# Two transformer blocks on one core: the norms between stages rebuilt, with the root of four of them applied behind the up products

## The chip, the cores and the metric

The kernel runs on one core of one Trainium2 chip. The core's engines are TensorE (PE, with its weight loads PEld), VectorE (DVE), ScalarE (ACT), GpSimd (POOL) and SyncE (SP), which issues the DMAs. The metric is the device time of one launch in microseconds. The clock granted to TensorE (PEclk) is given as a share of its full 2.4 GHz.

## The reference

Inputs are x (256 tokens of width 1024), a conditioning vector c, and weights. All is in float32. What matters here:

```python
def rms_norm(x, g):
    return x * rsqrt(mean(x * x, -1) + EPS) * g

# first half: layers 0 and 1
mod = silu(c) @ ada_w[l] + ada_b[l]              # 9 vectors of 1024 for each layer
h = rms_norm(x, g) * (1 + sc1) + sh1
x = x + 0.5 * g1 * swiglu(h)                     # feed-forward, 1024 -> 2 x 2816 -> 1024
h = ...;  x = x + g2 * (hybrid(h) if l == 0 else nsa(h))
h = ...;  x = x + 0.5 * g3 * swiglu(h)
# between the halves
x = rms_norm(x, final_g)
# second half: layers 0 and 1
f = (silu(rms_norm(x, g_pre) @ w_gate) * (rms_norm(x, g_pre) @ w_up)) @ w_down
x = x + 0.5 * rms_norm(f, g_post)
x = x + rms_norm(conformer(h) if l == 0 else diff_attention(h), g_post)   # h = rms_norm(x, g_pre)
x = x + 0.5 * rms_norm(f, g_post)                # a second feed-forward
```

There are 12 stages with a product in them: six in the first half (norms 0 to 5, feed-forwards 0 to 3, a hybrid of convolution and attention, an nsa attention) and six in the second (norms 6 to 11, feed-forwards 4 to 7, a conformer convolution, a differential attention). Norms 6, 8, 9 and 11 stand ahead of feed-forwards 4, 5, 6 and 7.

## The kernel before

Activations are kept with features on the partitions: `x`, `hf`, `h_hi` and `h_lo` are 128 x 8 chunks x 256 tokens. Weights come from memory as slabs of 128 x 2048 (1 MB), through three slots `raw`, `hi`, `lo`. ScalarE copies `raw` to `hi` in the rounded type of the matmuls, VectorE subtracts to get the rest `lo`, and every product is three matmuls (`mm3`): hi by hi, hi by lo, lo by hi. The activations are split the same way. Each engine runs its own program in a fixed order written out by hand, and semaphores join them. At the end of a stage `ahead()` splits the next stage's first two slabs, in front of the add.

A feed-forward has 11 steps. A step takes a gate slab and an up slab (`up`, into the two PSUM banks `AB[:, A]` and `AB[:, B]`, 48 matmuls each), and the down slab of the step before (`down`, into `Y`, 48 matmuls). ScalarE applies silu to bank A as soon as both banks are done, VectorE multiplies by bank B (`gate_mul`), and both split the product into `g_hi` and `g_lo` (in the last step `z_hi` and `z_lo`). The first step's `up` goes through the chunks of the first slab as they become ready; then four matmuls with zeros clear `Y` (L552), and the next `up` waits for the first gate product. In feed-forwards 0 to 3 VectorE also works on the ada product: `mac` multiplies 2 MB of weights by c (eight operations over 512 columns, L1256 and L1259), `cols` on TensorE sums over the partitions (L481), and `mod_out` stores the result. Pair `q0` is done before step 1, the others at the ends of the steps.

A norm goes so: ScalarE squares eight chunks into `hf` (L911; L974 for the result in `Y`; L979), GpSimd adds them in pairs (L845), and TensorE multiplies each pair sum by a column of ones, for the two halves of the tokens into banks `M` and `N` (L499). That is the statistic. VectorE computes the root with a seed from the bits and three Newton steps of three operations each (`rsqrt`, L1324 to L1329), TensorE spreads it over the partitions into `N` (L504, four records), and VectorE multiplies chunk by chunk (L1366), ScalarE writes `h_hi`, VectorE writes `h_lo` (L1372, L1376). An `add` of the second half norms the result of the stage too: statistic over `Y`, root, spread, a copy of the spread to `rstd` (L1346), and then for each chunk `hf = (Y + bias) * rstd` (L1452) and `x = x + gate * hf` (L1458). The `gate` vector is written by VectorE at the start of the add (L1440). In the conformer GpSimd makes diagonal matrices (L855) after the pairs of norm 7.

The start of the add and of the norm on VectorE:

```python
                rstd_of(EPS)
                for k in range(KD + 1):
...
                        ins = nc.vector.scalar_tensor_tensor(hf[:, k, :], Y[:, k, :], bias, rstd[:, :],
                                                             ALU.add, ALU.mult)
```

## Time and profile before

| what | value |
|---|---|
| time, median of 3 runs | 2496.24 us (2495.17 to 2500.86) |
| span of the profiled execution | 2499.1 us (its own time is not listed apart from the span) |
| PE busy | 2260.6 us, 90% |
| DVE busy | 1496.0 us, 60% |
| ACT busy | 924.7 us, 37% |
| POOL busy | 128.4 us, 5% |
| mean granted TensorE clock | 0.926 |
| HBM read | 415.2 MB, 167 GB/s over the span |

The profile is of one execution. Times in rows are microseconds from the span's start unless marked ns. An operation's row gives start, duration, engine, line, and output and inputs by their names; in square brackets stands how long the engine had been idle before it and what released it. Matmuls overlap, so the time from one start to the next says more than a duration. An f32 matmul of the statistic or the spread shows as two records.

### The profile page before, as it was taken

Reading aid. Unit: us, or ns where it says so; the run is one execution under the profiler, and the core shown is the slowest. Engines: PE = TensorE matmul, PEld = TensorE weight load, DVE = VectorE, ACT = ScalarE, POOL = GpSimd, SP = SyncE. Lnnn points to the kernel's source line nnn. Section 1 sums busy time; section 2 is a strip of 40 time slices with the busy share of each in tenths; the row PEclk is TensorE's granted clock in tenths of the full one; section 3 lists DMA queues with packets and bytes.
Section 4 is the critical chain, followed back from the end, with each engine's and each line's share of the span. In section 5 each row is a group of like instructions: output and inputs, shape, how many; then the busy total and the mean of one; then the engine's idle time right before and its main releaser. Section 6 shows DMA issues by size and latency. Waiting matters only on the chain.

```text
span 2499.1 us, 41640 instructions
## 1 busy us (share of the span) xinstructions
PE 2260.6 (90%) x17518; PEld 2208.7 (88%) x17518; DVE 1496.0 (60%) x2025; ACT 924.7 (37%) x1161; POOL 128.4 (5%) x92
## 2 busy tenths in 40 slices
PE   3999868999999999999989988779998998977997
PEld 3999768999899898889979988779997997967997
DVE  7776765776776536574454458954445446475444
ACT  2333433333333444343433333133343433433332
POOL 0000000000000000000000014510000001001000
PEclk9999888999999878899989988879998998988999
DMA  7776432776575332045525542115552552502552
GB/s 277 277 287 250 169 125 112 287 291 263 218 298 223 140 115 84 34 169 185 185 104 185 184 149 85 68 53 183 185 185 102 184 185 110 185 10 86 185 184 84
DMA packets 52499, 417.42 MB, mean 167 GB/s; under 512 B 5824, under 2 KB 5952, under 8 KB 6208
## 3 DMA queue, kind: packets, MB, share of 16 engines
q1 hardware_dynamic: 52416, 416.27, 44.8%
q8 instruction: 57, 0.93, 0.1%
q14 instruction: 26, 0.21, 0.0%
HBM read 415.20 MB, written 1.05 MB: 167 GB/s over the span
## 4 chain that ended last, share of the span: by engine, by line
PE 83%; DVE 12%; ACT 2%; issue 2%; POOL 1%; DMA 1%; SPq 0%; DVEq 0%; POOLq 0%; ACTq 0%
PE AB L252 17%; PE AB L253 17%; PE AB L254 17%; PE Y L252 8%; PE Y L254 8%; PE Y L253 8%; DVE lo L1230 2%; PE Y L660 2%; DVE ada_acc L1259 1%; PE M L481 1%; PE N L504 1%; PE M L691 1%; POOL hf L845 1%; DVE qT L1730 1%; PE Y L675 1%
## 5 line engine op out<-in xcount | busy, mean ns | idle before, releaser
L1230 DVE TENSOR_TENSOR lo<-raw,hi 128x2048 fp32r<-128x2048 f32 x322 | 747.1, 2323 | 591.4 <-ACT hi L883 591.2
L252 PE MATMUL AB<-h_hi,hi 128*128 128x256 f32 x3328 | 970.7, 292 | 27.7 <-DVE h_lo L1372 11.1
L253 PE MATMUL AB<-h_lo,hi 128*128 128x256 f32 x3328 | 956.1, 287 | 0.0
L254 PE MATMUL AB<-h_hi,lo 128*128 128x256 f32 x3328 | 955.3, 287 | 0.0
L883 ACT ACTIVATE hi<-raw 128x2048 fp32r<-128x2048 f32 x322 | 613.9, 1910 | 574.9 <-PE Y L254 303.4
L252 PEld LDWEIGHTS AB<-h_hi,hi 128*128 128x128 f32 x3328 | 651.3, 196 | 37.3 <-issue 19.5
L253 PEld LDWEIGHTS AB<-h_lo,hi 128*128 128x128 f32 x3328 | 654.7, 197 | 0.1
L254 PEld LDWEIGHTS AB<-h_hi,lo 128*128 128x128 f32 x3328 | 653.6, 196 | 0.0
L252 PE MATMUL Y<-g_hi,hi 128*128 128x256 f32 x1280 | 362.2, 283 | 0.0
L253 PE MATMUL Y<-g_lo,hi 128*128 128x256 f32 x1280 | 362.2, 283 | 0.0
L254 PE MATMUL Y<-g_hi,lo 128*128 128x256 f32 x1280 | 362.2, 283 | 0.0
L252 PEld LDWEIGHTS Y<-g_hi,hi 128*128 128x128 f32 x1280 | 245.8, 192 | 0.0
L253 PEld LDWEIGHTS Y<-g_lo,hi 128*128 128x128 f32 x1280 | 245.8, 192 | 0.0
L254 PEld LDWEIGHTS Y<-g_hi,lo 128*128 128x128 f32 x1280 | 245.8, 192 | 0.0
L1259 DVE SCALAR_TENSOR_TENSOR ada_acc<-ada_raw,cact,ada_acc 128x512 f32<-128x512 f32 x245 | 185.6, 758 | 8.7
L845 POOL TENSOR_TENSOR hf<-hf 128x256 f32<-128x256 f32 x80 | 68.3, 862 | 2312.8 <-ACT hf L911 1100.6
L1384 DVE TENSOR_TENSOR gf<-silu,AB 128x512 f32<-128x512 f32 x88 | 60.3, 685 | 193.3 <-ACT silu L949 133.2
L949 ACT ACTIVATE silu<-AB 128x512 f32<-128x512 f32 x80 | 47.8, 597 | 331.7 <-PE AB L254 331.7
L499 PE MATMUL M<-ones,hf 128*128 128x1 f32 x166 | 38.4, 300 | 49.4 <-POOL hf L845 47.9
L499 PEld LDWEIGHTS M<-ones,hf 128*128 128x128 f32 x166 | 32.8, 246 | 56.7 <-POOL hf L845 55.2
L481 PEld LDWEIGHTS M<-one,ada_acc 128*128 128x128 f32 x288 | 39.7, 211 | 46.1 <-DVE ada_acc L1259 30.1
L481 PE MATMUL M<-one,ada_acc 128*128 128x1 f32 x288 | 38.9, 256 | 44.7 <-DVE ada_acc L1259 44.7
(270 smaller groups left out, 2337.6 us busy)
## 6 DMA issues: line engine op xcount, KB each, us to landing
raw<-slabs SPq DMA_DIRECT2D x322, 1024.0 KB, 4.8
ada_raw<-ada SPq DMA_DIRECT2D x35, 2048.0 KB, 8.1
x<-x_t SPq DMA_DIRECT2D x1, 1024.0 KB, 10.2
kT<-ada SPq DMA_DIRECT2D x1, 1024.0 KB, 18.6
vt<-ada SPq DMA_DIRECT2D x1, 1024.0 KB, 20.6
out_t<-x SPq DMA_DIRECT2D x1, 1024.0 KB, 3.9
vec<-vectors SPq DMA_DIRECT2D x1, 462.0 KB, 3.5
hf<-constants SPq DMA_DIRECT2D x1, 401.0 KB, 15.2
```

Of the source, the lines that this page charges most:

```text
L252: nc.tensor.matmul(out_, w_hi, r_hi, start=start, stop=False, **kw)
L253: nc.tensor.matmul(out_, w_hi, r_lo, start=False, stop=False, **kw)
L254: return nc.tensor.matmul(out_, w_lo, r_hi, start=False, stop=stop, **kw)
L481: mm = nc.tensor.matmul(M[:, j:j + 1], ada_acc[:, j * P:(j + 1) * P], one[:, 0:1], start=True, stop=True)
L499: mm = nc.tensor.matmul((M, N)[t][:, 0:1], hf[:, base + every * k, t * P:(t + 1) * P], ones_[:, 0:1], start=(k == 0), stop=(k == n_chunks ...
L660: nc.tensor.matmul(out_, q_ap, k_ap, start=True, stop=not bias)
L845: nc.gpsimd.tensor_tensor(hf[:, k, :], hf[:, k, :], hf[:, k + 1, :], ALU.add).then_inc(pair_ready, 1)
L883: nc.scalar.activation(hi[slot][:, :], raw[slot][:, :], ACT.Copy).then_inc(hi_done[slot], 1)
L949: nc.scalar.activation(silu[:, :], AB[:, A, :], ACT.Silu).then_inc(silu_done, 1)
L1230: nc.vector.tensor_tensor(lo[slot][:, :], raw[slot][:, :], hi[slot][:, :].bitcast(F32), ALU.subtract).then_inc(lo_done[slot], 1)
L1259: nc.vector.scalar_tensor_tensor(ada_acc[:, :], w[k], cact[:, k:k + 1], ada_acc[:, :], ALU.mult, ALU.add).then_inc(ada_mac, 1)
L1384: nc.vector.tensor_tensor(gf[:, :], silu[:, :], AB[:, B, :], ALU.mult).then_inc(gf_done, 1)
```

## The change

- **Statistic.** GpSimd's four pair sums become a tree: chunks 0 to 3 are summed into one, 4 and 5 into one, 6 and 7 stay apart (`tree`). TensorE takes four parts (`stat_tree`): the sum of four, the sum of two, and the last two squares. Both token halves go to columns of one bank, `M`. Norms 7 and 10 are summed by TensorE from all eight squares, without GpSimd (`stat(KD, ones[1024])`).
- **Root.** `root_of` reads both columns at once; each Newton step is two operations instead of three, done for each token half by an instruction of its own.
- **Adds of the second half.** ScalarE squares each bank of `Y` into `ysq` (which is `kT`) and then writes `hf = gate * Y` for that bank; for this it waits once for VectorE's gate vector. VectorE multiplies `hf` by the spread, which it reads from `N` with no copy, and adds to `x`. The final norm reads `N` too.
- **Deferred norms** (6, 8, 9 and 11). `h = x * g` without the root: ScalarE writes `h_hi` from `x`, then the square; VectorE writes `h_lo` in the loop of the add (`low_half`). A reduction on VectorE sums the squares over chunks (`square_sum`), TensorE sums over the partitions after the first two slabs, the root follows, and its spread stands between the halves of the third slab. In every step VectorE multiplies both up products by the root (`gate_scaled`), and ScalarE's silu reads the scaled one.
- **First slabs.** In all stages the first two slabs are multiplied together, chunk by chunk (`by_chunk`). In feed-forwards they go into banks of `Y`. The next `up` no longer waits for the first gate product, and the first `down` starts the sums in `Y`, with no matmuls by zero.
- **Order.** In step 1 of a feed-forward the next up slab is split ahead of silu and the gate product. `mac` and `mod_out` stand between the gate product and the split of the down slab, in every step; the first `mac` is in step 1, and `cols` comes one step later.
- **Output.** Four DMAs of two chunks each instead of one.

```diff
+        DEFERRED = (6, 8, 9, 11)
+        def y_bank(b):
+            return Y[:, 2 * b:2 * b + 2, :].rearrange("p k t -> p (k t)")
 SyncE:
+                for k in range(0, KD, 2):
+                    sp.wait_ge(x_new, c["x_new"] - KD + k + 2)
+                    sp.dma_start(out[:, k:k + 2, :], x[:, k:k + 2, :]).then_inc(stored, 16)
 TensorE:
+            def stat_tree(sq):
+                s0, p0 = c.take("sq", KD), c.take("pair", 4)
+                sums([(pair_ready, p0 + 3, sq[:, 0, :]), (pair_ready, p0 + 4, sq[:, 4, :]),
+                      (sq_ready, s0 + 7, sq[:, 6, :]), (sq_ready, s0 + 8, sq[:, 7, :])], ones[1024])
+                spread()
+            def by_chunk(banks):
+                js = [c.take("slab") for _ in banks]
+                for k in range(KD):
+                    wait_h(k)
+                    for j, bank in zip(js, banks):
+                        s_ = j % 3
+                        if k == 0:
+                            pe.wait_ge(lo_done[s_], j // 3 + 1)
+                        for cc in range(2):
+                            at = k * 2 * P + cc * P
+                            mm = mm3(bank[:, cc * T:(cc + 1) * T], hi[s_][:, at:at + P], lo[s_][:, at:at + P],
+                                     h_hi[:, k, :], h_lo[:, k, :], k == 0 and cc == 0, k == KD - 1,
+                                     skip_group_check=True)
+                        if k == KD - 1:
+                            mm.then_inc(used[s_], 1)
             def ffn(f):
-                for ab in range(2):
-                    j = c.take("slab")
-                    pe.wait_ge(lo_done[j % 3], j // 3 + 1)
-                    up(ab == 0, ab, j % 3)
-                for b in range(4):
-                    nc.tensor.matmul(Y[:, 2 * b:2 * b + 2, :].rearrange("p k t -> p (k t)"), zero_b[:, 0:P],
-                                     zero_b[:, :], start=True, stop=False, skip_group_check=True)
+                by_chunk([y_bank(0), y_bank(1)])
+                if f >= 4:
+                    sums([(acc_ready, f - 3, rstd)], ones[1024])
+                pe.wait_ge(lo_done[ring[0][0]], ring[0][1] + 2)
+                up(0, ring[0][0], between=spread if f >= 4 else None)
+                pe.wait_ge(lo_done[ring[1][0]], ring[1][1] + 2)
+                up(1, ring[1][0])
+                pe.wait_ge(lo_done[ring[2][0]], ring[2][1] + 2)
+                pe.wait_ge(glo_done, g0 + 1)
+                down(ring[2][0], first=True)
 GpSimd:
+            def tree(sq):
+                pool.wait_ge(sq_ready, s0 + 2)
+                nc.gpsimd.tensor_tensor(sq[:, 0, :], sq[:, 0, :], sq[:, 1, :], ALU.add).then_inc(pair_ready, 1)
+                pool.wait_ge(sq_ready, s0 + 4)
+                nc.gpsimd.tensor_tensor(sq[:, 2, :], sq[:, 2, :], sq[:, 3, :], ALU.add).then_inc(pair_ready, 1)
+                pool.wait_ge(pair_ready, p0 + 2)
+                nc.gpsimd.tensor_tensor(sq[:, 0, :], sq[:, 0, :], sq[:, 2, :], ALU.add).then_inc(pair_ready, 1)
+                pool.wait_ge(sq_ready, s0 + 6)
+                nc.gpsimd.tensor_tensor(sq[:, 4, :], sq[:, 4, :], sq[:, 5, :], ALU.add).then_inc(pair_ready, 1)
+                if kind == "norm" and a[0] >= 6:
+                    c.take("sq", KD)
 ScalarE:
             def norm(n):
+                if n in DEFERRED:
+                    for k in range(KD):
+                        act.wait_ge(x_new, c["x_new"] - KD + k + 1)
+                        nc.scalar.activation(h_hi[:, k, :], x[:, k, :], ACT.Copy, scale=g[:, k:k + 1]
+                                             ).then_inc(hh_ready, 1)
+                        nc.scalar.activation(hf[:, k, :], x[:, k, :], ACT.Square).then_inc(sq_ready, 1)
+                    return
             def add(n):
+                    for b in range(KD // 2):
+                        result_bank(act, c, n, b)
+                        for k in (2 * b, 2 * b + 1):
+                            nc.scalar.activation(ysq[:, k, :], Y[:, k, :], ACT.Square, bias=bias).then_inc(sq_ready, 1)
+                        if b == 0:
+                            act.wait_ge(gate_done, n - 5)
+                        for k in (2 * b, 2 * b + 1):
+                                nc.scalar.activation(hf[:, k, :], Y[:, k, :], ACT.Copy, scale=gate[:, k:k + 1]
+                                                     ).then_inc(yg_ready, 1)
 VectorE:
+            def root_of(eps, scale=None):
+                link(nc.vector.tensor_scalar(vh, M[:, 0:TT], eps, -0.5, ALU.add, ALU.mult))
+                link(nc.vector.tensor_scalar(root[:, :].bitcast(I32), vh.bitcast(I32), -0.5, RSQRT_SEED,
+                                             ALU.mult, ALU.add))
+                for step in range(3):
+                    for t in range(TT):
+                        nc.vector.scalar_tensor_tensor(tmp[:, t:t + 1], y, y, vh[:, t:t + 1], ALU.mult, ALU.mult
+                                                       ).then_inc(dve_link, 1)
+                    for t in range(TT):
+                        dve.wait_ge(dve_link, at + t + 1)
+                        nc.vector.scalar_tensor_tensor(y, tmp[:, t:t + 1], 1.5, y, ALU.add, ALU.mult)
+            def gate_scaled(g, a_bank, b_bank, slot_b, n_b):
+                dve.wait_ge(used[slot_b], n_b)
+                dve.wait_ge(glo_done, g)
+                for to, from_ in ((silu, a_bank), (gf, b_bank)):
+                    nc.vector.tensor_tensor(..., from_, rstd broadcast, ALU.mult)
+                dve.wait_ge(silu_done, g + 1)
+                nc.vector.tensor_tensor(gf[:, :], gf[:, :], silu[:, :], ALU.mult).then_inc(gf_done, 1)
             def step(...):
+                    if first:
+                        split(sb_, i + nb)
+                    if first and f >= 4:
+                        dve.wait_ge(rstd_ready, c["stat"])
+                        link(nc.vector.tensor_copy(rstd[:, :], N[:, 0:T]))
                     gate_scaled(...) or gate_mul(...)
+                    if not first:
+                        split(sb_, i + nb)
+                    if out_:
+                        mod_out(i + (q0 - 2))
+                    if mac_:
+                        mac(0, i + (q0 - 1), i + (a0 - 1))
                     split(sw, i + nw)
                     gate_lo(i + (g0 - 1))
-                    if out_:
-                        mod_out(i + (q0 - 1))
                     if a:
                         split(sa, i + (na + 1))
-                    if mac_:
-                        mac(0, i + q0, i + a0)
             def add(n):
+                rstd_of(EPS, copy=False)
+                for k in range(KD + 2):
+                    if k < KD:
+                        nc.vector.tensor_tensor(hf[:, k, :], hf[:, k, :], N[:, 0:T], ALU.mult)
+                    if 1 <= k <= KD:
+                        nc.vector.tensor_tensor(x[:, k - 1, :], x[:, k - 1, :], hf[:, k - 1, :], ALU.add)
+                    if n + 1 in DEFERRED and k >= 2:
+                        low_half(n + 1, k - 2)
```

## Rows read from the trace of the kernel before

**Rows 1.** The page: granted clock in 40 slices, and the chain that ended last
```profile
PEclk9999888999999878899989988879998998988999
...
PE 83%; DVE 12%; ACT 2%; issue 2%; POOL 1%; DMA 1%; SPq 0%; DVEq 0%; POOLq 0%; ACTq 0%
```

**Rows 2.** Windows: stretch, length, busy us by engine, PEclk, DMA share, GB/s
```profile
1268.30:1288.00 19.70, 8.76 (x42) 7.58 (x41) 11.76 (x43) 6.46 (x17) 6.14 (x8) 0.62 0.16 64
1655.40:1676.30 20.90, 8.42 (x41) 7.34 (x40) 12.57 (x45) 4.98 (x12) 4.55 (x6) 0.58 0.11 45
1871.30:1891.70 20.40, 8.46 (x42) 7.39 (x41) 12.21 (x45) 4.80 (x12) 4.41 (x6) 0.56 0.15 60
1891.70:1906.20 14.50, 14.50 (x97) 14.39 (x97) 6.94 (x14) 4.31 (x7) 0.00 (x0) 0.79 0.20 73
2268.10:2288.00 19.90, 7.95 (x42) 6.94 (x40) 12.24 (x45) 4.80 (x12) 4.35 (x6) 0.63 0.12 49
1302.20:1470.00 167.80, 167.18 (x1390) 166.41 (x1390) 79.27 (x49) 65.41 (x49) 0.00 (x0) 1.00 0.50 181
```

**Rows 3.** Timeline of PE, between feed-forwards 5 and 6
```profile
1872.97 0.38 PE L499 MATMUL M<-ones,hf 128*128 128x1 f32 x2 [0.32 <-POOL hf L845]
1873.21 0.36 PE L499 MATMUL N<-ones,hf 128*128 128x1 f32 x2
1875.93 1.22 PE L504 MATMUL N<-ident,root 128*128 128x128 f32 x4 [2.36 <-DVE root L1329]
...
1882.48 0.59 PE L499 MATMUL M<-ones,hf 128*128 128x1 f32 x2 [0.58 <-POOL hf L845]
1882.93 0.57 PE L499 MATMUL N<-ones,hf 128*128 128x1 f32 x2
```

**Rows 4.** Timeline of DVE, the same stretch
```profile
1867.65 2.29 DVE L1230 TENSOR_TENSOR lo<-raw,hi 128x2048 fp32r<-128x2048 f32 x1 [0.18 <-ACT hi L883]
1869.86 0.71 DVE L1440 TENSOR_SCALAR gate<-vec 128x8 f32<-128x8 f32 x1
...
1877.19 0.42 DVE L1346 COPY rstd<-N 128x256 f32<-128x256 f32 x1 [1.31 <-PE N L504]
...
1878.32 0.47 DVE L1458 SCALAR_TENSOR_TENSOR x<-hf,gate,x 128x256 f32<-128x256 f32 x1
1878.72 0.42 DVE L1452 SCALAR_TENSOR_TENSOR hf<-Y,rstd 128x256 f32<-128x256 f32 x1
1879.05 0.48 DVE L1458 SCALAR_TENSOR_TENSOR x<-hf,gate,x 128x256 f32<-128x256 f32 x1
```

**Rows 5.** Timeline of ACT, the last squares of the add there
```profile
1871.46 0.66 ACT L974 ACTIVATE hf<-Y 128x256 f32<-128x256 f32 x2 [0.78 <-PE Y L254]
```

**Rows 6.** Timeline, where the last down product of feed-forward 3 begins
```profile
1261.57 0.69 DVE L1388 TENSOR_TENSOR z_lo<-gf,z_hi 128x512 fp32r<-128x512 f32 x1
...
1262.49 0.28 PE L252 MATMUL Y<-z_hi,hi 128*128 128x256 f32 x1
```

**Rows 7.** Timeline of PE, feed-forward 4 behind its first 96 matmuls
```profile
1302.27 1.04 PE L552 MATMUL Y<-zero_b 128*128 128x512 bf16 x4
1303.92 0.39 PE L252 MATMUL AB<-h_hi,hi 128*128 128x256 f32 x1 [0.62 <-DVE gf L1384]
```

**Rows 8.** Timeline, norm 7: a diagonal beside a Newton step
```profile
1499.38 2.56 POOL L855 TENSOR_TENSOR ot<-ident,vec 128x1408 f32<-128x1408 f32 x1
1499.48 2.47 DVE L1327 TENSOR_TENSOR var<-var,root 128x2 f32<-128x2 f32 x1
```

**Rows 9.** Timeline of DVE, feed-forward 1 ahead of step 1
```profile
432.75 5.48 DVE L1259 SCALAR_TENSOR_TENSOR ada_acc<-ada_raw,cact,ada_acc 128x512 f32<-128x512 f32 x7
```

**Rows 10.** The page: DMA issues, KB each, us to landing
```profile
out_t<-x SPq DMA_DIRECT2D x1, 1024.0 KB, 3.9
```

**Rows 11.** The chain near the program's start: start us, us, what
```profile
21.13 1.11 DVE ada_acc L1259
```

**Rows 12.** Groups of DVE in the differential attention, 2112 to 2265
```profile
L1786 DVE TENSOR_REDUCE rec<-hf 128x8 f32<-128x1024 f32 x2 | 2.4, 1220 | 0.1
```

More of the change, by code:

```diff
@@ L275, in program @@
                     for kind, *_ in plan)
+        SQ_DONE, n_sq = {}, 0
+        for kind, *a in plan:
+            if kind in ("norm", "final", "conformer") or kind == "add" and a[0] >= 6:
+                n_sq += KD
+            elif kind == "hybrid":
+                n_sq += 3
+            if kind == "norm":
+                SQ_DONE[a[0]] = n_sq
         ADA_FFN = {0: (4, 10), 1: (16, 10), 2: (26, 8), 3: (34, 2)}
@@ L614, in features @@
                     for k in range(KD):
[L615 removed]
+                        if paced and cc == 0:
                             wait_h(k)
@@ L753, in nsa @@
             def nsa():
-                for j in range(4):
-                    features(halves(result("a")), first=(j == 0))
+                by_chunk([result("a"), result("a")])
+                for j in (2, 3):
+                    features(halves(result("a")))
                 for j in (4, 5):
@@ L861, in _ @@
                     diagonals()
-                if kind in ("norm", "final", "conformer") or kind == "add" and a[0] >= 6:
-                    pairs()
+                if kind == "norm" and a[0] >= 6:
+                    c.take("sq", KD)
+                elif kind in ("norm", "final", "conformer"):
+                    tree(hf)
+                elif kind == "add" and a[0] >= 6:
+                    tree(ysq)
                 elif kind == "hybrid":
```

261 lines of the change are left out of this document (158 added, 103 removed).

## The prediction

> **What bounds the kernel now.** I read the page first. The chain that ended last is 83% TensorE and 12% VectorE, and the granted clock falls to eight or seven tenths in the slices where one stage gives way to the next [rows 1]. The windows say why. Inside the feed-forward loops TensorE is busy 167.2 of 167.8 us at the full clock, while VectorE does 79 us of work, so what is put on VectorE there lies beside matmuls. Between stages it is the reverse: from the last product of one stage to the first of the next 19.7, 20.9, 20.4 and 19.9 us pass before the four feed-forwards of the second half, with TensorE busy about 8 us of it, and on tiny matmuls [rows 2]. Then the PE and VectorE timelines of one such stretch (1871 to 1892): statistic, root, spread, copy, an add at 0.73 us a chunk, a second statistic, root and spread, and only then the first product [rows 3, 4].
>
> **The sum by stages.** I count from the last product of a stage (E) to the first of the next (S), from S to the end of its first 96 matmuls (F), and from F on.
>
> *Pieces that recur.* (a) Root: 2.36 us pass between statistic and spread [rows 3], for two evictions, a seed and nine dependent steps. The new chain has one eviction, a seed and three times two steps, each step a pair of small instructions that overlap; a dependent step costs 0.2 us (2.36 over 12, with the ends), the second of a pair about 0.08. That makes 1.9: -0.4 each. (b) The copy of the spread, 0.46 us with its wait [rows 4], goes in adds and in the final norm. (c) Statistic after the tree. GpSimd still makes four adds in a row, 0.77 us each (eight in 6.14 us [rows 2]), and the last ends when it did; but now three parts wait behind it in place of one. A part is two matmuls, 0.24 us apart at 2.4 GHz and 0.45 at 1.2 GHz [rows 3], so two more parts cost 0.9 or 1.8: I take +1.25. (d) In the adds of the second half the last two squares go straight to TensorE, without a GpSimd hop: -0.75 where banks come late. (e) But ScalarE now also scales each bank, and waits at bank 0 for the gate, which VectorE writes only at 1870.57, behind two slab splits [rows 4]. Twelve operations of 0.33 us [rows 5] then follow, so the last square ends near 1874.6 in place of 1872.1. With the next item the statistic of an add behind a feed-forward ends 2.0 later (not in the last add: no slab is split ahead there). (f) The last product of a feed-forward: z_lo ends 0.23 us before TensorE wants it [rows 6]; the scaling of the up products in front of it takes 0.7, so TensorE stands 0.6; this is within the +2.0.
>
> *Deferred norms.* The new norm waits for no second statistic: x, then h_hi on ScalarE, then h_lo. After the spread come three VectorE operations of 0.33 to 0.48, one of 0.42 on ScalarE and one more on VectorE: S is 2.45 us behind the spread (1.55 after the final norm, with one VectorE operation less). So E to S becomes:
> - before the second (after the conformer): 0.9 last squares + 0.5 + 1.9 + 1.2 spread + 2.45 = 7.0, against 20.9: -13.9.
> - third: 4.35 to the statistic's end (2.35 now, + 2.0 by (e)) + 1.9 + 1.2 + 2.45 = 9.9, against 20.4: -10.5.
> - fourth: 7.0 (spread nearer to 0.8), against 19.9: -13.0.
> - first: 4.8 to the statistic's end (3.9 now; (c) at full clock, +0.9) + 1.9 + 1.2 + 1.55 = 9.5, against 19.7: -10.2.
>
> Behind S the clock is at 1.2 GHz, as before: TensorE has then stood about as long as it did when the clock fell. The 96 matmuls take 14.5 us at a mean clock of 0.79 [rows 2], so 0.12 each at full clock, nearly twice that at half, and the clock rises some 6 us behind S. Chunk-outermost order gives TensorE 12 matmuls per chunk (1.44 us at full clock, over 2.5 at half) against a supply of one chunk per 1.1 us on VectorE (three operations), so it never waits for a chunk. But before, it did three per 0.73 us where three at half clock take 0.64 to 0.7: it hardly waited, and there is little to win. F is S + 14.0 against 14.5 [rows 2]: -0.3 to -0.6. At F the clearing matmuls and the wait for the first gate cost 1.65 us [rows 7]; now the sums (0.45) and the spread (0.7) stand there: -0.5 (last: -0.85, estimated). The reduction over the squares, the next slab's split and the root lie beside the 14 us; if that cover were gone, they would cost 2.2 + 2.3 + 1.9 a time. Together: first -11.0, second -14.9, third -11.5, fourth -14.2.
>
> *Inside those four loops.* Per step (`gate_scaled`) VectorE gets two more operations over 512 columns, 0.69 each like the z_lo of [rows 6], and the gate comes 2.9 us behind the up products (scale 0.7, silu 0.6 beside the second scale, product 0.7, with waits) in place of 1.5. The 48 down products, 5.8 us, lie between: nothing. VectorE's 9.7 us a step fit into TensorE's 17.3. Unseen is the price of such a product with a broadcast operand; bounds are 0.69 and, as in the stretched row of [rows 8], 2.5. At the upper one the chain is 2 x 2.5 + 0.7 and some waits, and just fills the cover. I take 0.69, the row with one operand in PSUM and the same shape.
>
> *First half.* In step 1 the ada accumulation now stands between the first gate product and the next split. From F: hi 2.0, split 4.3, gate 4.95, eight accumulations of 0.75 [rows 9] to 10.95, split 13.15, g_lo 13.85; TensorE is through its next two slabs at 11.5: it stands 2.4. The clearing matmuls and wait of 0.9 go: +1.5. In later steps g_lo is ready 15.9 us after the gate chain starts and due at 18.1. Stage by stage: first feed-forward +0.6 (chunk-outermost must also wait for the second slab, but an old stall of 6.5 us goes), hybrid 1.25 (c) - 0.4 (a) + 0.05 - 0.75 for its own two roots = +0.15; the second feed-forward 1.25 - 0.4 - 0.9 (F) + 1.5 = +1.45; the third the same with F at -0.5, +1.85; nsa 1.25 - 0.4 - 0.6 + 0.75 = +1.0 (both result banks end together, so the third slab waits 0.75 for a ScalarE copy); the fourth with F at -0.8, +1.55. Sum +6.6.
>
> *The rest.* Norm before the conformer: GpSimd's diagonals (2.56 each) hold VectorE's root for 3.4 us now [rows 8]; they only move ahead, to the root of the add before, since GpSimd has no squares to wait for there any more. Conformer: its two first results end together, so its taps, which bound it, start 2.9 later; with (e), (c) and what is saved +1.3 in all. Diff: +0.4. Last add: statistic -0.75 + 0.6, root and copy -0.85, adds -0.35, and the output in four pieces instead of one of 3.9 us [rows 10]: -1.5; sum -2.9.
>
> Total: 6.6 - 11.0 + 1.3 - 14.9 - 11.5 + 0.4 - 14.2 - 2.9 = -46.2 us. The profiled execution spans 2499.1, so 2452.9 in such an execution; its span lies 2.9 above the median of the three runs, so 2450 for a median.
>
> **A rule against the change.** In [rows 4] the product that reads PSUM (L1452) lets its successor start after 0.33 us, no later than the one with all inputs in SBUF does (L1458, 0.40). The Trainium skill, VectorE: DVE Perf Modes, section on the TRN2 errata, gives VectorE 58 cycles of fixed cost from SBUF and 120 from PSUM. By that each of the products that now read the spread from PSUM would pay some 0.065 us more (an estimate from that page), 0.5 an add: the copy's saving would be gone, 3 us in all. The row decides here.
>
> **Rivals.**
> - *The clock does not fall* in the shorter pauses. For it: they shrink from 20 us to 7 to 10. Against it: in [rows 3] the spread, 4.8 us behind the last product, already runs at 1.2 GHz (1.22 us for four). Worth 28 x 0.09 = 2.6 us each and more for the spreads: about 2439.
> - *The accumulation comes too late in every first-half step.* Slack is 2.2 us. If an accumulation takes 1.1 us rather than 0.75, as at the start of the program [rows 11], TensorE stands 0.6 in 27 steps: 2466.
> - *The reduction is slow.* It reads 2048 elements with a stride. Nearest row: 1.22 us for 1024 in order [rows 12], so 2.2 to 2.4. At four times that it and the splits behind it end some 5 us after F: 4 x 5, so 2470.
> - *Slower.* The gate chain of the deferred loops becomes the bound: it decides from the point where the chain from the up products to the gate exceeds the 5.8 us of down products. To end above 2496 each of 40 steps must stand 1.2 us, so the chain must take 7.0, over twice my 2.9; with both scalings at the stretched 2.5 it is 5.8, not enough. With all three products at 2.5 it is 7.6, TensorE stands 1.8 in each step, and the time is 2450 + 72 = 2522. For it: the two last products have two operands in SBUF. Against it: GpSimd, beside which the stretched row ran, is idle in these loops [rows 2].
> - *It does nothing on the path*: the deferred products still wait for the root. Only if the order on VectorE put the root ahead of the chunks; it stands behind them. 2492.
>
> **How the numbers follow.** Forecast 0.64 (own range 2440 to 2460, from (c), (e) and where the clock rises), clock 0.09, accumulation 0.10, reduction 0.08, slower 0.04, nothing 0.05. The predicted time is that of the first; low 2436 takes in the clock, high 2468 the accumulation and most of the reduction. A measurement here tells 0.2% (5 us) from nothing. Faster: 0.64 + 0.09 + 0.10 + 0.08 + 0.02 = 0.93; same 0.03 (2492 lies near the bound, so its 0.05 is shared 2 to 3); slower 0.04.
>
> **What would show it.** First products before the four feed-forwards 7 to 10 us behind the last one; no clearing matmuls; first gate at F without a stop of TensorE in the second half and a stop of 2.4 us before the first down product in the first half; last statistic three parts long; ScalarE waiting for the gate at bank 0; root 1.9. It is wrong if TensorE's idle time in the second-half loops grows, or if the clock rises much later than 6 us behind S.

## The result and the profile after

The changed kernel takes 2531.18 us in the median of 4 runs (2526.72 to 2541.8), the kernel before 2495.99 beside it. The ratio is 1.015, with a 95% interval of 1.0128 to 1.0171: slower by 1.5%, where I forecast 2450 us and a gain. The profiled execution spans 2524.9 us, 25.8 more than that of before; my sum said 46.2 less.

By the end of the last product of each stage, the 25.8 come from opposite sides. The first half, up to feed-forward 3, is 65.8 us longer (forecast: 6.6). Its feed-forwards lost 25.3, 23.5, 18.5 and 6.3 us, with 10, 10, 8 and 2 ada accumulations; hybrid and nsa gained 1.6 and 6.3. The second half is 39.9 us shorter (forecast: 52.8): feed-forwards 4, 5, 6 and 7 gained 9.4, 9.7, 10.1 and, with the end, 13.3 us (forecast: 11.0, 14.9, 11.5 and 17.1); the conformer lost 2.9 and diff gained 0.3.

The page of the kernel after, its chain that ended last (to be read against [rows 1]):

```profile
PE 59%; DVE 20%; DMA 10%; ACT 5%; issue 4%; POOL 1%; SPq 1%; DVEq 0%; ACTq 0%
PE AB L259 10%; PE AB L261 10%; PE AB L260 10%; DMA raw<-slabs 10%; DVE ada_acc L1357 7%; PE Y L259 6%; PE Y L260 6%; PE Y L261 6%; DVE lo L1328 4%; ACT hi L954 4%; DVE qT L1903 2%; PE M L524 2%; PE Y L721 2%; PE Y L736 1%; PE M L752 1%
```

TensorE had 83% of that chain before and has 59% now. New in it are slab loads (10%) and the accumulation (7%). The waits after, first PE's, then ACT's, then those of SP's queue (us in total, times, longest):

```profile
PE Y L259 <- DVE g_lo L1535: 53.0, 30, 2.9
...
ACT hi L954 <- DMA raw<-slabs: 249.2, 53, 10.5
...
SPq L418 <- DVE lo L1328: 1822.4, 292, 101.9
SPq L428 <- DVE ada_acc L1357: 462.4, 29, 30.1
```

and SP's in the kernel before:

```profile
SPq L392 <- DVE lo L1230: 2050.5, 318, 109.0
SPq L402 <- DVE ada_acc L1259: 207.8, 29, 29.5
```

Read them from the bottom up. SP issues every load, in one fixed order. Its 29 ada loads used to wait 207.8 us for accumulations; they now wait 462.4. ScalarE then waits 249.2 us for slabs, a wait that is in none of the longest of before, and TensorE stands 30 times, 53.0 us, ahead of a down product. There are 30 accumulations in the feed-forwards: one stop for each. Four of the stops are in first steps, 1.5 us each; 26 are in later steps.

One such step, in feed-forward 1. The chain that ended last, 480 to 503, then DVE, SP, ACT and PE, then the step as a window (length, busy us by engine, PEclk, DMA share, GB/s):

```profile
472.45 9.33 DMA raw<-slabs
481.81 1.92 ACT hi L954
...
493.10 10.73 DMA raw<-slabs
```

```profile
483.75 2.29 DVE L1328 TENSOR_TENSOR lo<-raw,hi 128x2048 fp32r<-128x2048 f32 x1 [6.80 <-ACT hi L954]
...
486.03 0.48 DVE L1354 TENSOR_SCALAR ada_acc<-ada_raw,cact 128x512 f32<-128x512 f32 x1
486.55 5.48 DVE L1357 SCALAR_TENSOR_TENSOR ada_acc<-ada_raw,cact,ada_acc 128x512 f32<-128x512 f32 x7
491.94 2.28 DVE L1328 TENSOR_TENSOR lo<-raw,hi 128x2048 fp32r<-128x2048 f32 x1
494.14 0.68 DVE L1535 TENSOR_TENSOR g_lo<-gf,g_hi 128x512 fp32r<-128x512 f32 x1
...
505.80 2.29 DVE L1328 TENSOR_TENSOR lo<-raw,hi 128x2048 fp32r<-128x2048 f32 x1 [8.17 <-ACT hi L954]
...
492.22 0.33 SPq L428 DMA_DIRECT2D ada_raw<-ada  x1
493.10 4.43 SPq L418 DMA_DIRECT2D raw<-slabs  x3
...
503.86 1.91 ACT L954 ACTIVATE hi<-raw 128x2048 fp32r<-128x2048 f32 x1 [10.53 <-DMA raw<-slabs]
...
494.97 0.36 PE L259 MATMUL Y<-g_hi,hi 128*128 128x256 f32 x1 [2.28 <-DVE g_lo L1535]
```

```profile
480.13:502.28 22.15, 19.87 (x154) 19.70 (x153) 13.63 (x14) 6.86 (x5) 0.00 (x0) 0.92 0.67 267
```

The split of slab b at 483.75 ends at 486.04 and frees its slot, so the reload could start. But SP's next entry is the ada load, and that waits for the accumulation behind the split. It goes out at 492.22, the slab's reload at 493.10, 7 us late and behind 2 MB of ada weights, so that it needs 10.73 us, where the median of all slab loads is 4.8. ScalarE gets the slab at 503.86 after 10.53 us of nothing, VectorE splits it at 505.80, and the accumulation of that step starts as late again. The accumulation does not take longer (5.48 for seven, as in [rows 9]). It begins late, and g_lo is 2.28 us late with it. Then comes the clock: the step's mean is 0.92. Its 22.15 us are 4.0 more than the 18.16 that a step takes in e1 below, 2.3 by standing and the rest by half clock.

This step is not the usual one. From one `g_lo` to the next the first three feed-forwards take 20.4 to 20.9 us in 24 of 25 cases, with the slab's load at 9.2 to 9.6; the one of 22.1 is where that load takes 10.73. Later in the same feed-forward TensorE stands as long, at full clock (the row of one stop, and the step behind it up to the end of the next stop):

```profile
599.52 0.36 PE L259 MATMUL Y<-g_hi,hi 128*128 128x256 f32 x1 [2.48 <-DVE g_lo L1535]
...
599.50:620.10 20.60, 18.41 (x153) 18.26 (x153) 13.66 (x15) 6.86 (x5) 0.00 (x0) 1.00 0.64 258
```

So what sets the pace is a ring without TensorE in it: the ada load goes out, 0.9 us later the slab load (9.3), then come ScalarE's copy (1.9), VectorE's split (2.3), the accumulation (6.1), and the next ada load. It takes 20.6 us against TensorE's 18.2.

### The profile page after: what moved, and what is told of

The parts are those of the page before. It is cut to its first block, busy times and chain, and to the rows that moved or that the text cites. A ratio compares the mean times of both kernels' runs of the same rounds, so it can differ in the third digit from the quotient of the medians.

```text
span 2524.9 us, 41719 instructions
## 1 busy us (share of the span) xinstructions
PE 2252.9 (89%) x17470; PEld 2207.7 (87%) x17470; DVE 1547.4 (61%) x2128; ACT 946.2 (37%) x1209; POOL 113.2 (4%) x68
## 4 chain that ended last, share of the span: by engine, by line
PE 59%; DVE 20%; DMA 10%; ACT 5%; issue 4%; POOL 1%; SPq 1%; DVEq 0%; ACTq 0%
PE AB L259 10%; PE AB L261 10%; PE AB L260 10%; DMA raw<-slabs 10%; DVE ada_acc L1357 7%; PE Y L259 6%; PE Y L260 6%; PE Y L261 6%; DVE lo L1328 4%; ACT hi L954 4%; DVE qT L1903 2%; PE M L524 2%; PE Y L721 2%; PE Y L736 1%; PE M L752 1%
## 5 line engine op out<-in xcount | busy, mean ns | idle before, releaser
L259 PE MATMUL AB<-h_hi,hi 128*128 128x256 f32 x3072 | 880.7, 287 | 12.6 <-DVE ada_raw L1913 5.8
L260 PE MATMUL AB<-h_lo,hi 128*128 128x256 f32 x3072 | 875.1, 285 | 0.0
L261 PE MATMUL AB<-h_hi,lo 128*128 128x256 f32 x3072 | 874.8, 285 | 0.0
L954 ACT ACTIVATE hi<-raw 128x2048 fp32r<-128x2048 f32 x322 | 614.6, 1910 | 645.3 <-DMA raw<-slabs 249.2
L260 PEld LDWEIGHTS AB<-h_lo,hi 128*128 128x128 f32 x3072 | 595.9, 194 | 0.1
L259 PE MATMUL Y<-h_hi,hi 128*128 128x256 f32 x512 | 156.3, 305 | 27.0 <-DVE h_lo L1469 8.4
L260 PE MATMUL Y<-h_lo,hi 128*128 128x256 f32 x512 | 154.0, 301 | 0.0
L261 PE MATMUL Y<-h_hi,lo 128*128 128x256 f32 x512 | 153.4, 300 | 0.0
L259 PEld LDWEIGHTS Y<-h_hi,hi 128*128 128x128 f32 x512 | 108.1, 211 | 29.7 <-DVE h_lo L1469 9.5
L260 PEld LDWEIGHTS Y<-h_lo,hi 128*128 128x128 f32 x512 | 108.1, 211 | 0.0
L261 PEld LDWEIGHTS Y<-h_hi,lo 128*128 128x128 f32 x512 | 107.7, 210 | 0.0
## 6 DMA issues: line engine op xcount, KB each, us to landing
x<-x_t SPq DMA_DIRECT2D x1, 1024.0 KB, 10.1
vt<-ada SPq DMA_DIRECT2D x1, 1024.0 KB, 20.4
```

Source lines behind the costliest of these rows:

```text
L259: nc.tensor.matmul(out_, w_hi, r_hi, start=start, stop=False, **kw)
L260: nc.tensor.matmul(out_, w_hi, r_lo, start=False, stop=False, **kw)
L261: return nc.tensor.matmul(out_, w_lo, r_hi, start=False, stop=stop, **kw)
L954: nc.scalar.activation(hi[slot][:, :], raw[slot][:, :], ACT.Copy).then_inc(hi_done[slot], 1)
```

## Experiments

All times are medians, all ratios against the kernel before, run beside them on the same chip. Runs e1 to e4 share one chip, e5 to e8 a second, e9 and e10 a third; across these groups the ratios compare better than the times.

| run | us | ratio, 95% interval |
|---|---|---|
| e1_load_order | 2460.32 | 0.9841 (0.9817 to 0.9864) |
| e2_old_accumulation | 2456.66 | 0.9826 (0.9810 to 0.9843) |
| e3_before_new_accumulation | 2565.64 | 1.0267 (1.0246 to 1.0287) |
| e4_gate_early | 2520.96 | 1.0082 (1.0065 to 1.0099) |
| e5_both_mended | 2447.09 | 0.9798 (0.9768 to 0.9827) |
| e6_pairs | 2436.81 | 0.9759 (0.9735 to 0.9782) |
| e7_not_deferred | 2482.46 | 0.9955 (0.9936 to 0.9973) |
| e8_slab_order | 2449.40 | 0.9807 (0.9784 to 0.9831) |
| e9_chunk_order_where_deferred | 2431.24 | 0.9734 (0.9714 to 0.9754) |
| e10_squares_first | 2428.16 | 0.9727 (0.9707 to 0.9747) |

### The loss of the first half: e1, e2, e3

**e1**, in SP's program of the changed kernel:

```diff
                 def step(i, ada, a):
                     load(sb_, i * 3 + (j0 - 2), i + nb)
+                    if ada:
+                        load_ada(0, i + (q0 - 1), i * KD + KD * (q0 - 1))
                     load(sw, i * 3 + (j0 - 1), i + nw)
                     if a:
                         load(sa, i * 3 + j0, i + (na + 1))
-                    if ada:
-                        load_ada(0, i + q0, i * KD + KD * q0)
...
-                for flags, run in groupby(range(1, NSTEP), lambda i: (i < n_ada, i < NSTEP - 1)):
+                for flags, run in groupby(range(1, NSTEP), lambda i: (2 <= i <= n_ada, i < NSTEP - 1)):
```

> The changed kernel with one edit in SP's list of loads: in a feed-forward step the load of the modulation slab stands behind the load of slab b and ahead of those of w and a, as the subtractions and the accumulation now follow each other on DVE, instead of behind all three. Theory (the modulation load, which waits for the accumulation that now lies in the middle of DVE's step, holds up the reload of slab b behind it in SP's queue by about 6.5 us): the steps with modulation go from 22.15 us back to about 18.2, the three waits of some 2.3 us a step go, and with the 1.7 us that stay in each first step the time is about 2527 - 60 = 2467 us (2460 to 2475). Rival one (the accumulation itself is too late for the product of the same step, the slack of 2.2 us that the prediction left being too small, whatever SP does): the wait for g_lo stays at some 1.8 us in 28 steps and the time is 2505 to 2527. Rival two (the loads of other queues or the DMA engines' share are short): nothing moves, 2527.

2460.32 us: the theory, at the lower edge of its range, and 71 us below the changed kernel by the medians (68.6 by the profiled spans), by one entry moved in one queue. PE's wait for g_lo in the whole kernel, and one step of feed-forward 1 as a window:

```profile
PE Y L259 <- DVE g_lo L1535: 6.0, 4, 1.5
```

```profile
481.66:499.82 18.16, 18.16 (x154) 18.16 (x153) 13.88 (x15) 7.68 (x6) 0.00 (x0) 1.00 0.78 300
```

The 26 stops outside the first steps are gone, with 47.0 us of waiting; the four in first steps stay, at 1.5. Up to the last product of feed-forward 3 the trace is 67.25 us shorter. In TensorE's time that is the 47 of standing and 20 of half clock, which had stood behind 12 of the 26 stops; in cause it is the ring, some 2.45 us a step in 26 steps, an estimate of 64 us. The two don't add to each other, for where the clock had fallen the next stop was mostly shorter (2.22 us, then 1.04, in feed-forward 0) and the pace was the same. That half now takes 1.5 us less than before the change. The rival that the slack of 2.2 us was too small falls: the same order on VectorE, with loads on time, lets TensorE run through.

**e2**: `mac`, `cols` and `mod_out` at their old places, and with them `mac(0, q0, a0)` ahead of step 1. VectorE's part, without its loop bounds:

```diff
-                    if out_:
-                        mod_out(i + (q0 - 2))
-                    if mac_:
-                        mac(0, i + (q0 - 1), i + (a0 - 1))
                     split(sw, i + nw)
                     gate_lo(i + (g0 - 1))
+                    if out_:
+                        mod_out(i + (q0 - 1))
                     if a:
                         split(sa, i + (na + 1))
+                    if mac_:
+                        mac(0, i + q0, i + a0)
```

> The changed kernel with the modulation's accumulation, its columns and its read-out put back where they were before (one accumulation ahead of the first step, then at the end of each step); SP's list is untouched, and all else of the change stays. Theory (the whole loss of the first half hangs on where the accumulation stands): both that loss of 66 us and the wait of 1.7 us in each first step go, about 2527 - 66 = 2461 us (2452 to 2468). Rival (the chunk-outermost first slabs, the written-out first step or the statistic cost part of the first half): 2470 or more, with the rest of the loss left in the feed-forwards of the first half. The second half should stay as it is in the changed kernel, 40 us shorter than before.

2456.66 us, as the theory has it, and within 4 us of e1, which their intervals do not tell apart. What the new place was good for can't be seen in the time: with either order in agreement with SP's, the loops run at TensorE's pace.

**e3**: the same lines the other way round, put into the kernel before.

> The kernel before with that one part of the change: the accumulation, its columns and its read-out at their new places on DVE and PE, SP's list untouched. Theory: it alone makes the loss, 2497 + 60 = 2557 us (2545 to 2570), with steps of about 22 us in the first three feed-forwards. Rival (the loss needs the new first step or the slabs in chunk order as well): 2497 to 2515.

2565.64 us, inside the theory's range and 2.7% slower than before, with nothing else of the change. The wait is the same one in the same number:

```profile
PE Y L252 <- DVE g_lo L1388: 56.5, 30, 2.9
```

So the place of the accumulation, against an SP list that was not moved with it, is both needed for the loss and enough for it.

### The second half: e4 and e5

From here on a product's end is its start plus the 0.12 us to the next start. The add behind the conformer in the changed kernel; ACT, DVE, POOL, PE, with the last product ending at 1714.65:

```profile
1710.90 0.82 ACT L1063 ACTIVATE kT<-Y,vec 128x256 f32<-128x256 f32 x2
1714.19 1.02 ACT L1068 ACTIVATE hf<-Y,gate_bias,gate 128x256 f32<-128x256 f32 x2 [2.46 <-DVE gate_bias L1604]
...
1718.33 0.90 ACT L1063 ACTIVATE kT<-Y,vec 128x256 f32<-128x256 f32 x2
...
1711.03 2.29 DVE L1328 TENSOR_TENSOR lo<-raw,hi 128x2048 fp32r<-128x2048 f32 x1 [3.47 <-ACT hi L954]
1713.24 0.71 DVE L1603 TENSOR_SCALAR gate<-vec 128x8 f32<-128x8 f32 x1
...
1711.81 2.12 POOL L907 TENSOR_TENSOR kT<-kT 128x256 f32<-128x256 f32 x1 [32.98 <-ACT kT L1063]
1716.02 0.72 POOL L909 TENSOR_TENSOR kT<-kT 128x256 f32<-128x256 f32 x1 [2.10 <-ACT kT L1063]
...
1723.35 1.22 PE L533 MATMUL N<-ident,root 128*128 128x128 f32 x4 [2.19 <-DVE root L1450]
1726.81 0.58 PE L259 MATMUL Y<-h_hi,hi 128*128 128x256 f32 x1 [2.24 <-DVE h_lo L1469]
```

ScalarE stands 2.46 us for the gate, behind a mixer too. Its last two squares end at 1719.2, 4.6 us behind the last product, where I had put 0.9. In e4 the gate vector is written at the start of the stage (`gate_vector`, with the lines taken from the start of `add`; its definition is left out here):

```diff
                 step(1, y_bank(0), y_bank(1), (j0 - 1) % 3, (j0 - 1) // 3 + 1, False, n_ada > 0, True, first=True)
+                if f >= 4:
+                    gate_vector(3 * (f // 2) + 2 * (f % 2))
...
             def conformer():
+                gate_vector(7)
...
             def diff():
+                gate_vector(10)
```

> The changed kernel with one edit: in the second half the gate vector is written at the start of the stage and not behind DVE's splits for the next one. Theory (each addition's scaled copies, and behind them the last squares, wait about 2.5 us for the gate, behind the mixers too, which the prediction left out): each of the six additions ends its statistic 2 to 2.5 us sooner, about 2527 - 13 = 2514 us (2510 to 2517), and E to S becomes about 7.5 to 8 us in all three feed-forward to mixer transitions. Rival (the squares then wait for the copies between them, or POOL's tree is what ends last): 0.5 to 1 us for each, 2521 to 2525.

2520.96 us, 10 below the changed kernel. That misses the theory's 2510 to 2517 and lies at the rival's 2521. The trace says otherwise about the size: the second half is 12.8 us shorter than in the changed kernel, the theory's 13, while the first half of this execution is 9.6 longer, with no edit there and a cause that stays open. From the last product to the first the second, third and fourth feed-forward now take 8.66, 8.92 and 8.51 us, after 12.16, 11.26 and 10.22; ahead of the conformer and diff 1.6 less each. That is not the 7.5 to 8 I wrote, and e4's rows of the same add say why; it is what the rival named, the copies between the squares and the tree:

```profile
1721.99 1.08 ACT L1068 ACTIVATE hf<-Y,gate_bias,gate 128x256 f32<-128x256 f32 x2
1722.89 0.91 ACT L1063 ACTIVATE kT<-Y,vec 128x256 f32<-128x256 f32 x2
...
1722.62 2.18 PE L524 MATMUL M<-ones,kT 128*128 128x1 f32 x16 [0.66 <-POOL kT L911]
```

The last product ended at 1721.80, but its squares wait for the copies of the bank before (until 1722.89), and then two of the four parts are still to come at half clock, until 1724.8.

**e5** has the edits of e1 and e4.

> The changed kernel with the load order of e1 and the early gate vector of e4 together. Theory (two causes in different halves, which add up): 2460 - 10 = 2450 us (2446 to 2454). Rival (the early gate vector gives part back, as the first step of a feed-forward has less room once the loads are on time): 2454 to 2460.

2447.09 us: the two causes add up. This is the change as it could have been, near my 2450, in part by luck. By halves the trace has +4.4 and -51.2 us against my +6.6 and -52.8, but the terms err both ways: the stretches from last product to first are 10.4, 8.7, 8.5 and 8.7 us where I had 9.5, 7.0, 9.9 and 7.0.

### The statistic: e6

e5 with pair sums on GpSimd and four parts, each as its pair is ready:

```diff
-                sums([(pair_ready, p0 + 3, sq[:, 0, :]), (pair_ready, p0 + 4, sq[:, 4, :]),
-                      (sq_ready, s0 + 7, sq[:, 6, :]), (sq_ready, s0 + 8, sq[:, 7, :])], ones[1024])
+                sums([(pair_ready, p0 + k + 1, sq[:, 2 * k, :]) for k in range(4)], ones[1024])
```

> e5 with the statistic's tree put back to pair sums (four sums of two on GpSimd, four parts on TensorE, each as its pair is ready; both token halves stay in one bank). Theory (the tree's tail of three parts on TensorE, which lasts 2.05 us from 1925.6 to 1927.64 in the trace of e4, costs more than a last sum of 0.73 and one part of 0.7 behind the last square): 0.9 us less for each of 13 statistics, 2438 us (2434 to 2444). Rival one (the sum's term (c) was 0.9 to 1.8 only beside late squares, and the squares and GpSimd set the end either way): 2447 to 2452. Rival two (the tree is the better order where squares come late, as the change has it): 2453 or more.

2436.81 us, as the theory has it; the two intervals overlap a little, so the rows carry the rest. The statistic between feed-forwards 5 and 6, on PE, in e5 (last product until 1854.31):

```profile
1854.89 2.28 PE L524 MATMUL M<-ones,kT 128*128 128x1 f32 x16 [0.43 <-POOL kT L911]
```

and in e6 (until 1847.82):

```profile
1847.82 1.39 PE L524 MATMUL M<-ones,kT 128*128 128x1 f32 x12
1849.53 0.61 PE L524 MATMUL M<-ones,kT 128*128 128x1 f32 x4 [0.32 <-POOL kT L907]
```

The tree ends 2.9 us behind the last product, the pairs 2.3, and the root follows. Last product to first goes from 8.53 to 7.87 here, from 9.73 to 8.38 ahead of feed-forward 2; behind the conformer it went from 8.66 to 9.53, and there the tree is the better one: the last squares end 2.0 us behind the last product, and a sum on GpSimd still follows. Behind diff, where they end 0.9 behind it, the pairs are better again (8.67 to 7.46, of it 0.5 by a spread at full clock).

### What deferring is worth: e7

e5 with the norms not deferred; every branch `f >= 4`, but for the one that writes the gate vector, goes as this one:

```diff
-        DEFERRED = (6, 8, 9, 11)
+        DEFERRED = ()
...
-                if f >= 4:
+                if f >= 40:
                     sums([(acc_ready, f - 3, rstd)], ones[1024])
```

> e5 with the four norms ahead of the feed-forwards of the second half done in front of them, as the two norms ahead of the mixers are (statistic from all eight squares on TensorE, root, spread, multiply, split), and no scaling of up products. Theory (deferring is worth the second statistic, root and spread in each of these four transitions, about 11 us each, and nothing is given back in the loops): from the last product to the first 19 to 20.5 us in place of 8.5 to 9.5, and 2450 + 46 = 2496 us (2490 to 2502). Rival (the scalings cost some 0.3 us in each of 40 steps, so that undoing gives 12 us back): 2484.

2482.46 us, 35 over e5: the rival's number and not the theory's 46. Windows of e5, from the last product of the conformer (0.12 us behind its end as taken above) to the first of the next stage, and on to its 192nd matmul:

```profile
1651.51:1660.05 8.54, 3.36 (x21) 2.86 (x21) 4.17 (x21) 3.87 (x10) 1.32 (x2) 0.73 0.30 115
1660.05:1686.40 26.35, 26.35 (x199) 26.35 (x200) 22.81 (x42) 13.72 (x20) 0.00 (x0) 0.89 0.25 82
```

and of e7:

```profile
1653.37:1673.17 19.80, 11.57 (x57) 10.69 (x56) 10.69 (x48) 6.86 (x17) 1.33 (x2) 0.58 0.13 50
1673.17:1697.90 24.73, 24.73 (x192) 24.73 (x193) 15.10 (x20) 11.06 (x12) 0.00 (x0) 0.92 0.37 129
```

Ahead of the first product deferring wins 11.3 us. Behind it 1.6 us are given back by the 192nd matmul (0.8 of it by the 96th, the rest for the sums and the spread that stand between); in the other three stages it is 1.2, 1.1 and 0. By the end of the stages it is 1.9, 2.4, 1.9 and 0.75. So the rival had the number by the wrong mechanism: it is not 0.3 us in each of 40 steps. At the 288th matmul the gap is still 1.66; in the loop the scalings are hidden. They show once, at the end of each of the four stages, where the gap grows by 0.75 and TensorE waits for z_lo, which it does not in e7. The row is of the changed kernel, with 0.52 in all four stages there and in e5:

```profile
1915.05 0.36 PE L259 MATMUL Y<-z_hi,hi 128*128 128x256 f32 x1 [0.52 <-DVE z_lo L1535]
```

The four stages win 45 and give back 7. The conformer and diff, whose code is the same, take 1.4 and 1.7 us less in e7, for a cause that stays open. That leaves the 35 of the medians.

### Chunk order: e8, e9, and e10

**e8**: in `by_chunk` the loop over slabs is the outer one, then that over the two column halves, and the chunks are inside.

> e5 with the first two slabs of every stage multiplied one after the other, each chunk of the first as it is ready, in place of chunk by chunk in both. Theory (one chunk every 1.1 us from VectorE in the deferred stages against three matmuls of 0.65 to 0.7: about 3 us of waiting in four stages; in the others, at 0.73 a chunk, 0.3 to 0.6): 2450 + 12 + 4 = 2466 us (2460 to 2470). Rival (TensorE's clock rises no later either way and the waits only fill time that the half clock would take): 2450 to 2455.

2449.40 us, level with e5: far below the theory's 2460 to 2470 and next to the rival's 2450. The theory was right about its own stages and the sum was still near zero. The first 96 matmuls of feed-forward 5:

```profile
1648.09:1664.60 16.51, 16.29 (x96) 14.81 (x97) 12.30 (x20) 8.86 (x16) 0.00 (x0) 0.74 0.16 59
```

16.5 us in place of 14.0 in e5; 1.3, 2.5, 2.9 and 3.3, so 10.0 over the four deferred stages (the 9.2 in the expectation of e9 is too low). Against that, the first feed-forward starts without waiting for its second slab and ends 5.2 sooner than in e7, which has e5's code there. From their first product on, feed-forwards 1 to 3 take 1.3, 0.8 and 1.3 less than in e7, and the conformer 2.4 less than in e5 but only 0.7 less than in e7.

**e9** keeps chunk order only in feed-forwards 4 to 7, on top of e6; the mixers call `by_slab` too.

```diff
-                by_chunk([y_bank(0), y_bank(1)])
+                (by_chunk if f >= 4 else by_slab)([y_bank(0), y_bank(1)])
```

> e6 with chunk order of the first two slabs kept only ahead of the four feed-forwards with a deferred norm; in all other stages one slab follows the other, as in e8. Theory (e8 came out level because two effects cancel: slab order costs 1.3 to 2.9 us in each deferred stage, where a chunk comes every 1.06 us, 9.2 in all, and saves 5.2 in the first feed-forward, which need not wait for the second slab, 3.4 in the other three and 2.4 in the conformer): 2437 - 11 = 2426 us (2421 to 2431). Rival (the order matters to neither, and e8's level time is just that): 2434 to 2440.

2431.24 us: in the direction of the theory, at half its size, and just over the edge of its range. Its interval overlaps that of e6, so the step alone is not settled by time.

**e10**, on top of e9, in ScalarE's part of `add`:

```diff
-                        if b == 0:
+                        if b == 2:
                             act.wait_ge(gate_done, n - 5)
-                        for k in (2 * b, 2 * b + 1):
+                        for k in {0: (), 1: (), 2: (0, 1), 3: range(2, KD)}[b]:
```

> e9 with ScalarE's order in the six additions of the second half changed: the squares of banks 0 to 2, the scaled copies of bank 0, the squares of bank 3, then the other copies, in place of squares and copies bank by bank. Theory (behind the mixers, where three banks are ready at once, the last square waits 1.0 us for copies; behind feed-forwards the banks come 1.44 us apart, as long as ScalarE's work on one, and nothing waits): 1 us less in two additions, 2424 us (2421 to 2427). Rival (the copies then come too late for VectorE's products behind the spread, so that it costs more than it saves): 2428 or more.

2428.16 us, outside the theory's range and on the rival's edge; the intervals can't tell it from e9, so no gain is shown by time. In the traces the stretch behind the conformer goes from 9.11 to 8.15 us, as foretold. The one behind diff, foretold too, stays at 7.97. The one behind feed-forward 5 goes from 7.46 to 7.97, but not by the order: the statistic ends 2.3 us behind the last product in both, and the spread, which takes 1.22 us in e10, is at full clock in e9:

```profile
1839.64 0.71 PE L533 MATMUL N<-ident,root 128*128 128x128 f32 x4 [2.19 <-DVE root L1460]
```

By its median e10 is the fastest version of this study, 2.7% under the kernel before. It keeps the deferred norms and the adds without a copy; load order, place of the gate, statistic, chunk order and order of the squares are amended.

## Why the prediction was wrong

**The step that failed** is that of the first half: "In later steps g_lo is ready 15.9 us after the gate chain starts and due at 18.1", costed at nothing. That sum took VectorE's inputs for given. What feeds it is SP's queue, past which the accumulation was moved: the ada load stands ahead of slab b's reload and waits for an accumulation that used to be over by then and is now in the middle of the step. The prediction wrote down what VectorE does with each slab and never what SP does when VectorE's order changes. e1 and e3 show it from both sides: it is the 59 of the first half, out of the 72 us by which the sum's span was missed. In place of nothing it cost 67 us, as the step's ring of loads takes 20.6 us where TensorE needs 18.2. The other 13 are in the second half.

My rival "the accumulation comes too late in every first-half step" names the place and the symptom. Its mechanism (1.1 us per accumulation) and its 2466 were both wrong, since at 0.75 the accumulation was as fast as ever. With loads on time there is no stop.

**Step 1 of the first half**: stop of 2.4 forecast, 1.5 measured, four times. Right in kind.

**(e), the late gate**, was seen for feed-forwards and left out for the adds behind mixers, where I put the last square 0.9 us after the last product; it was 4.6. The gate costs 10 to 13 us in all (10 by e4's median; 12.8 by the second half of its trace, 9.9 by that of e5 against e1), of which my sum held about 6 (2.0 in each of three adds).

**(a), the root**: -0.4 forecast, -0.17 measured: 2.19 between statistic and spread against the 2.36 of [rows 3]. In part this is a wrong sum: eight steps of 0.2 and six seconds of 0.08 make 2.1 and not 1.9. The rows show a pair as one group, and the time from a group to the next is what counts:

```profile
1721.19 0.16 DVE L1437 TENSOR_SCALAR var<-M 128x2 f32<-128x2 f32 x1 [7.04 <-PE M L524]
1721.39 0.17 DVE L1438 TENSOR_SCALAR root<-var 128x2 int32<-128x2 int32 x1
1721.59 0.35 DVE L1443 SCALAR_TENSOR_TENSOR var<-root,var 128x1 f32<-128x1 f32 x2
1721.86 0.28 DVE L1450 SCALAR_TENSOR_TENSOR root<-var,root 128x1 f32<-128x1 f32 x2
1722.17 0.35 DVE L1443 SCALAR_TENSOR_TENSOR var<-root,var 128x1 f32<-128x1 f32 x2
```

A Newton step takes 0.58 (1721.59 to 1722.17), two pairs of 0.29. Before, three single operations took 0.59 (1874.15 to 1874.74). Only the second eviction was saved.

**(c), the tree**: +1.25 forecast at about every statistic. e6 says about +0.8 (10 us by the medians over 13 statistics; 0.6 by the spans), just below my 0.9 to 1.8. Right in kind, sized a little high. With (a) it means that the tree costs and the new root saves little where banks come on time.

**(f), z_lo**: 0.6 forecast, 0.52 measured, four times.

**Deferred norms**: the first product comes 2.24 behind the spread's end, 2.45 forecast; in the loops the gate chain is hidden, and so are the reduction and the root; the first down product needs no clearing. All of that is as forecast, so the rival that it does nothing on the path falls. E to S was 11.20, 12.16, 11.26 and 10.22 against 9.5, 7.0, 9.9 and 7.0, the last three by (e), (a) and the copies between the squares, the first by the tree's parts at half clock (it is 9.39 with the pairs of e6). The gate chain of the second step of feed-forward 5:

```profile
1754.12 0.68 DVE L1525 TENSOR_TENSOR silu<-AB,rstd 128x512 f32<-128x512 f32 x1
1754.72 0.68 DVE L1525 TENSOR_TENSOR gf<-AB,rstd 128x512 f32<-128x512 f32 x1
1755.59 0.69 DVE L1531 TENSOR_TENSOR gf<-gf,silu 128x512 f32<-128x512 f32 x1 [0.19 <-ACT silu L1029]
```

The broadcast operand costs nothing extra: 0.68, the lower of my two bounds, so the rival that this chain becomes the bound falls. (The row of [rows 6] that I took it from has both operands in SBUF and not one in PSUM, as I wrote; it made no difference.) The rival on the clock falls in the changed kernel, as a spread still takes 1.22 us (1723.35, above); in the shorter stretches of e6 and e9 one spread each was at full clock, 0.71. That of the slow reduction falls too: it is slow but hidden (below).

**The rest**: conformer +2.9 against +1.3, diff -0.3 against +0.4.

The rule that I weighed against the change does not show. The product that reads the spread from PSUM (L1622) lasts as long as the add with both inputs in SBUF (L1626) and lets its successor start as soon:

```profile
1725.61 0.41 DVE L1622 TENSOR_TENSOR hf<-hf,N 128x256 f32<-128x256 f32 x1
1725.94 0.42 DVE L1626 TENSOR_TENSOR x<-x,hf 128x256 f32<-128x256 f32 x1
```

In the rows above an operation of 128 x 2 that reads PSUM (L1437) lasts 0.16 and one that reads SBUF (L1438) 0.17. By the Trainium skill, VectorE: DVE Perf Modes, section on the TRN2 errata, the one from PSUM should last 0.065 us longer, an estimate from its 58 and 120 cycles. No run here shows that.

## What to carry to other kernels

A queue whose entries each wait for another engine is part of that engine's order: when work moves in VectorE's program, put the loads that its end releases to the matching place in the issuing program, or everything behind them is late by the distance. In a slack sum, write next to each operation which load feeds it and what that load's issue waits for. Add up the whole ring from one such load to the next and compare it with the step, and not the slack of one engine alone. And a chain is as long as its starts are apart: pairs that overlap and copies between squares look free in busy time and were not.

## What the hardware showed that I had not expected

- The reduction over chunks (L1475, 128 x 256 from 128 x 2048, read with a stride) takes longer than the 2.2 to 2.4 I took from [rows 12], though far from the 9 at which it would show. It is hidden.

```profile
1733.39 3.87 DVE L1475 TENSOR_REDUCE rstd<-hf 128x256 f32<-128x2048 f32 x1
```

- GpSimd's first add of the tree lasts 2.12 us at 1711.81, beside VectorE's split of 1711.03 to 1713.3, and the next, with VectorE idle, 0.72. The stretch of [rows 8] is thus not peculiar to the diagonals. The Trainium skill, GPSIMD Engine Reference, section Specifications, says that GpSimd's way to SBUF contends with a VectorE instruction that has two SBUF inputs, which the split has; the trace agrees.
- TensorE's granted clock fell to 1.2 GHz around 12 of the 26 stops in later steps, the one of 2.28 us at 494.97 among them (mean of the step 0.92; 1.00 in e1, without the stop). It stayed at 2.4 GHz around the others, also around the 2.48 us at 599.52. TensorE had been busy for 18.2 us before either. The pace of the loop was 20.6 us both ways.
